# Rows by indirect DMA: a mixture of experts whose rows are fetched and summed in DRAM

## What is computed

```python
def swiglu(x, wg, wu, wd):
    return jnp.dot(jax.nn.silu(jnp.dot(x, wg)) * jnp.dot(x, wu), wd)

def moe_swiglu(x, router, wg, wu, wd):
    xf = x.reshape(-1, x.shape[-1])
    logits = jnp.dot(xf, router).astype(jnp.float32)
    top_v, top_i = lax.top_k(logits, TOP_K)
    probs = jax.nn.softmax(top_v, axis=-1)
    gate = jnp.sum(jax.nn.one_hot(top_i, N_EXPERTS) * probs[..., None], axis=1)
    y = jnp.zeros(xf.shape, jnp.float32)
    for e in range(N_EXPERTS):
        y = y + gate[:, e:e + 1] * swiglu(xf, wg[e], wu[e], wd[e])
    return y
```

## Time and profile before

| | |
|---|---|
| median of 3 runs | 1292.19 us (1291.65 to 1292.32) |
| the profiled execution | 1290.74 us, its span 1289.0 us |
| PE busy | 96% |
| DVE busy | 79% |
| ACT busy | 64% |
| DMA, mean | 258 GB/s |
| mean granted PE clock | 0.986 of full speed |

### The profile page before, as it was taken

One profiled execution on the slowest core, in us unless ns is written; L12 is line 12 of the kernel. 1 busy time (PEld: TensorE's weight loads), 2 busy tenths in 40 slices (PEclk: granted clock), 3 DMA queues, 4 the chain that ended last, 5 costly groups with the idle time before them and its releaser, 6 DMA issues.

```text
span 1289.0 us, 16501 instructions
## 1 busy us (share of the span) xinstructions
PE 1231.6 (96%) x6719; PEld 1066.7 (83%) x6719; DVE 1012.1 (79%) x977; ACT 818.6 (64%) x899; POOL 4.2 (0%) x20
## 2 busy tenths in 40 slices
PE   6999999999998899999999999999999999999993
PEld 4899999989998778878887887887887887887882
DVE  6687444457997678889889879879879979879875
ACT  3646563345776577767776776776776767767751
POOL 0000000000000000000000000000000000000000
PEclk8999999999999999999999999999999999999996
DMA  9145543434463169989998998998998998998931
GB/s 254 45 154 163 164 163 131 164 98 131 144 215 121 64 232 371 372 298 356 371 327 322 371 328 320 371 331 326 372 321 329 372 335 312 373 338 311 370 143 52
DMA packets 167645, 333.03 MB, mean 258 GB/s; under 512 B 6404, under 2 KB 58980, under 8 KB 167530
## 3 DMA queue, kind: packets, MB, share of 16 engines
q1 hardware_dynamic: 167363, 331.28, 72.9%
q10 hardware_dynamic: 199, 0.62, 0.2%
HBM read 330.44 MB, written 2.84 MB: 259 GB/s over the span
## 4 chain that ended last, share of the span: by engine, by line
PE 75%; DVE 20%; ACT 3%; issue 1%; DMA 0%; DVEq 0%; SPq 0%; ACTq 0%
PE bank L1145 29%; PE bank L1167 17%; PE bank L961 17%; DVE w_lo L1247 10%; PE bank L992 6%; DVE cacc L1430 2%; PE bank L1098 2%; ACT w_hi L569 1%; PE bank L1154 1%; PE bank L900 1%; DVE acc L1595 1%; DVE yy_lo L1665 1%; PE bank L946 1%; DVE sg L1327 1%; DMA xin<-in_x_prompt_dram 0%
## 5 line engine op out<-in xcount | busy, mean ns | idle before, releaser
L1247 DVE TENSOR_TENSOR w_lo<-raw,w_hi 128x2048 fp32r<-128x2048 f32 x309 | 703.7, 2289 | 145.6 <-ACT w_hi L569 145.4
L569 ACT CAST w_hi<-raw 128x2048 fp32r<-128x2048 f32 x309 | 590.1, 1918 | 251.7 <-PE bank L1145 93.7
L1145 PE MATMUL bank<-w_hi,xg_hi 128*128 128x512 f32 (+1 forms) x768 | 290.6, 378 | 1.1 <-DVE xg_lo L1602 1.1
L1145 PE MATMUL bank<-w_lo,xg_hi 128*128 128x512 f32 (+1 forms) x768 | 287.2, 374 | 0.0
L1145 PE MATMUL bank<-w_hi,xg_lo 128*128 128x512 f32 (+1 forms) x768 | 286.8, 373 | 0.0
L961 PE MATMUL bank<-x_hi,w_hi 128*128 128x304 f32 (+1 forms) x544 | 165.8, 305 | 6.9 <-DVE x_lo L1334 3.7
L1145 PEld LDWEIGHTS bank<-w_hi,xg_hi 128*128 128x128 f32 x768 | 144.7, 188 | 27.6 <-issue 1.3
L1145 PEld LDWEIGHTS bank<-w_hi,xg_lo 128*128 128x128 f32 x768 | 144.5, 188 | 26.7
L1145 PEld LDWEIGHTS bank<-w_lo,xg_hi 128*128 128x128 f32 x768 | 144.9, 189 | 25.2
L961 PE MATMUL bank<-x_hi,w_lo 128*128 128x304 f32 (+1 forms) x544 | 163.8, 301 | 0.0
L961 PE MATMUL bank<-x_lo,w_hi 128*128 128x304 f32 (+1 forms) x544 | 163.1, 300 | 0.0
(11 more groups left out here) (197 smaller groups left out, 1227.7 us busy)
## 6 DMA issues: line engine op xcount, KB each, us to landing
raw<-in_moe_w_gate_dram SPq DMA_DIRECT2D x88, 1024.0 KB, 5.4
raw<-in_moe_w_up_dram SPq DMA_DIRECT2D x88, 1024.0 KB, 5.4
raw<-in_moe_w_down_dram SPq DMA_DIRECT2D x88, 1024.0 KB, 5.3
raw<-in_conv_w_dram SPq DMA_DIRECT2D x12, 1024.0 KB, 5.5
raw<-in_ffn_w_gate_dram SPq DMA_DIRECT2D x11, 1024.0 KB, 5.3
raw<-in_ffn_w_up_dram SPq DMA_DIRECT2D x11, 1024.0 KB, 5.3
raw<-in_ffn_w_down_dram SPq DMA_DIRECT2D x11, 1024.0 KB, 4.9
poolw<-in_pool_w_dram SPq DMA_DIRECT2D x1, 1024.0 KB, 10.9
```

The lines of the kernel that those rows point to most:

```text
L569: act.copy(w_hi[t % HIGH][:], raw[raw_slot(t)][:]).then_inc(hi_ready, 1)
L1145: done = pe.matmul(bank[:, 0:w], x[:, f, :], m[:, c, :], start=(f == 0 and k == 0), stop=(f == KC - 1 and k == 2))
L1247: dve.tensor_tensor(w_lo[raw_slot(t)][:], raw[raw_slot(t)][:], w_hi[t % HIGH][:], ALU.subtract).then_inc(split_ready, 1)
```

## The change

- Rows are stored once, as `xn` in float32 (no hi and lo), to a DRAM tensor `rows_dram`, and `acc` (alpha times the rows) to `sums_dram`, which has 128 more rows for slots that no row fills. Both are stored by SP ahead of the load of expert tile 11.
- `sel` is made for all experts before the first one, in three parts. `find_rows` multiplies it with `gate`, whose columns are now a 1, the shares of the 8 experts and the row's number: each slot gets its row's number, its share, and whether it is filled. DVE turns these into `row_in` (row to fetch), `row_out` (row to add to) and `share`.
- For each expert, GpSimd fetches 128 rows by an indirect DMA into `xg_rows`. `gather_rows` and ACT's copies go; `gather_turn` waits for the DMA.
- `scatter`, `sel_t`, the splits of `yy` and the adds on DVE go. ACT writes `yy`, the result times `share`, and GpSimd adds it to the rows of `sums_dram` by an indirect DMA that accumulates. It is issued behind the fetch of the next expert but one, and each add waits for the one before. The last expert is left out.
- In the last expert, behind its last weight tile, SP loads `g_row`, `b_row` and the sums of the seven experts into `acc`; DVE and ACT norm all rows, at places in block 4, block 5 and behind, and SP stores all outputs. For the last expert's own slots GpSimd fetches the sums to `z_rows`; DVE adds `yy` times share, norms these 128 rows, and two indirect stores (one to each output, with a bound that drops the other's rows) write them over what SP stored.
- PE's last `down` finishes its first half (bank 6) six matmuls ahead of the second. ACT reads the flag before the first expert.

```diff
+            def store_rows():
+                for i in range(3):
+                    n = OUT_ROWS[i]
+                    sp.wait_ge(rows_copied, 2 * i + 2)
+                    sp.dma_start(rows_dram[P * i:P * i + n, :], xn[0:n, i, :]).then_inc(rows_stored, 16)
+                for i in range(3):
+                    n = OUT_ROWS[i]
+                    sp.wait_ge(acc_ready, 2 * i + 2)
+                    sp.dma_start(sums_dram[P * i:P * i + n, :], acc[0:n, i, :]).then_inc(sums_stored, 16)
+                sp.dma_start(sums_dram[NM:NM + P, :], acc[:, 0, :]).then_inc(sums_stored, 16)
...
+            def fetch(n, e):
+                pool.indirect_dma_start(xg_rows[:], None, rows_dram, rows(row_in[:, e:e + 1], 0)).then_inc(xg_landed, 16)
+
+            def add(n, e):
+                pool.wait_ge(yy_done, 2 * n + 2)
+                pool.indirect_dma_start(sums_dram, rows(row_out[:, e:e + 1], 0), yy[:], None,
+                                        compute_op=ALU.add).then_inc(added, 16)
+
+            pool.wait_ge(rows_stored, 48)
+            pool.wait_ge(in_ready, 1)
+            fetch(0, 0)
+            pool.wait_ge(in_ready, 3)
+            for e in range(1, E):
+                pool.wait_ge(gathered, 2 * e)
+                fetch(e, e)
+                if e == 2:
+                    pool.wait_ge(sums_stored, 64)
+                    pool.wait_ge(out_ready, 1)
+                elif e > 2:
+                    pool.wait_ge(added, 16 * (e - 2))
+                if e > 1:
+                    add(e - 2, e - 2)
+            pool.wait_ge(added, 16 * (E - 2))
+            add(E - 2, E - 2)
+            pool.wait_ge(added, 16 * (E - 1))
+            pool.wait_ge(rows_stored, 48)
+            pool.indirect_dma_start(z_rows[:], None, sums_dram, rows(row_out[:, E - 1:E], 0)).then_inc(z_landed, 16)
...
+            pool.wait_ge(y_stored, 48)
+            pool.wait_ge(rows_ready, 1)
+            pool.indirect_dma_start(y_prompt[0], rows(row_out[:, E - 1:E], 0), y_rows[:], None,
+                                    bounds_check=SEQ - 1, oob_is_err=False).then_inc(y_placed, 16)
+            pool.indirect_dma_start(y_sample.rearrange("b t d -> (b t) d"), rows(row_ys[:], 0), y_rows[:], None,
+                                    bounds_check=NS - 1, oob_is_err=False).then_inc(y_placed, 16)
...
+            def find_rows(r, k):
+
+                e0, e1, bank = FINDS[k]
+                pe.wait_ge(sel_ready, r * len(FINDS) + (k + 1))
+                for e in range(e0, e1):
+                    for i in range(3):
+                        n = OUT_ROWS[i]
+                        last = pe.matmul(ps[bank][:, GC * e:GC * (e + 1)], sel[0:n, e, i, :], gate[0:n, i, :],
+                                         start=(i == 0), stop=(i == 2))
+                last.then_inc(rows_found, 1)
...
                     rows_block(ps[2 + (j + 1) % 2], j, g + halves(j))
-                    if j == 1 and scatters:
-                        pe.wait_ge(summed, scattered + 4)
+                    if j == 1 and (not isinstance(n, int) or n > 0):
+                        pe.wait_ge(yy_done, n * 2)
                     if j:
-                        if j == NB - 1 and not last:
-                            gather_rows(n + 1)
                         down(j - 1, g + 2 * halves(j))
...
+                    if kept and j == NB - 1:
+                        for i in range(2):
+                            rows_center(0, i)
                     mult(j)
...
+                    if kept and j == NB - 2:
+                        dve.wait_ge(sums_loaded, 48)
+                        for i in range(3):
+                            rows_stats(0, i)
+                        dve.wait_ge(rows_landed, 32)
+                if kept:
+                    rows_center(0, 2)
+                    for i in range(2):
+                        rows_scale(0, i)
                 turn_low(NB - 1)
+                if kept:
+                    rows_scale(0, 2)
...
+            def last_rows():
+
+                dve.wait_ge(z_landed, 16)
+                for k in range(2):
+                    cols = slice(k * HALF, (k + 1) * HALF)
+                    if k == 0:
+                        dve.wait_ge(first_half, E)
+                    else:
+                        dve.wait_ge(tile_used, T_MOE + E * TE)
+                    dve.scalar_tensor_tensor(out=yy[:, cols], in0=ps[6 + k][:, :], scalar=share[:, E - 1:E],
+                                             in1=z_rows[:, cols], op0=ALU.mult, op1=ALU.add).then_inc(yy_done, 1)
...
```

More of the change, by code:

```diff
@@ L510, in _ @@
                     one_pass(r)
[L511 to L520, removed]
+                sp.wait_ge(added, 16 * 3 * E)
+                load_sums()
+                store_y(1)
+                sp.wait_ge(y_stored, 16 * 6)
             sp.wait_ge(u_stored, 16 * (1 + ST_))
-            sp.wait_ge(stored, 16 * (4 + 3))
+            sp.wait_ge(stored, 16 * 4)
+            sp.wait_ge(y_stored, 16 * 3)
+            sp.wait_ge(y_placed, 32)
         @block.gpsimd
@@ L554, in _ @@
+        N_CONSTS = 13
         @block.scalar
@@ L785, in one_expert @@
                 t0 = n * TE
+                kept = last and isinstance(r, int)
                 m0 = T_MOE + side * TE
@@ L857, in _ @@
                     one_pass(r)
[L859 to L862, removed]
+                all_rows_std(1)
         @block.tensor
@@ L1110, in gather_turn @@
                     last.then_inc(gathered, 1)
-            def scatter(y_count):
-                pe.wait_ge(yy_lo_done, y_count)
-                for k in range(6):
-                    i, half = k // 2, k % 2
-                    n = OUT_ROWS[i]
-                    for m, y in enumerate((yy_hi, yy_lo)):
-                        last = pe.matmul(ps[SCATTER_BANKS[k]][0:n, :], sel_t[:, P * i:P * i + n],
-                                         y[:, half * HALF:(half + 1) * HALF], start=(m == 0), stop=(m == 1))
-                    last.then_inc(spread, 1)
             def one_expert(r, first, side, last):
@@ L1577, in _ @@
             link(last)
+            for i in range(3):
+                last = dve.scalar_tensor_tensor(out=slot_of[:, i, 0:E], in0=ps[1][:, i * E:(i + 1) * E], scalar=1.0,
+                                                in1=taken[:, i, :], op0=ALU.add, op1=ALU.mult)
             for i in range(3):
@@ new lines, in _, with rows_stats, rows_center @@
+            output_rows(0)
+            def rows_stats(k, i):
+                n = OUT_ROWS[i]
+                for half in range(2):
+                    dve.bn_stats(stats[0:n, i, half, :],
+                                 acc[0:n, i, half * HALF:(half + 1) * HALF]).then_inc(fin_half, 1)
+                dve.wait_ge(fin_half, 6 * k + 2 * i + 2)
+                dve.bn_aggr(mv[0:n, i, :], stats[0:n, i, :, :].rearrange("p a b -> p (a b)")).then_inc(fin_stats, 1)
+            def rows_center(k, i):
+                n = OUT_ROWS[i]
+                dve.wait_ge(fin_stats, 3 * k + i + 1)
+                dve.scalar_tensor_tensor(out=acc[0:n, i, :], in0=acc[0:n, i, :], scalar=mv[0:n, i, 0:1],
+                                         in1=g_row[0:n, :], op0=ALU.subtract, op1=ALU.mult).then_inc(fin_g, 1)
@@ L1609, in one_expert @@
                 n = pair + side
-                e = first + side
-                scatters = not isinstance(n, int) or n > 0
                 m0 = T_MOE + side * TE
+                kept = last and isinstance(r, int)
                 def ahead(j):
```

367 lines of the change are left out of this document (208 added, 159 removed).

## The result

The changed kernel takes 1249.18 us (1248.36 to 1249.45) where the kernel before took 1291.92: a ratio of 0.9669, with a 95% interval of 0.9653 to 0.9686, or 42.7 us less. The forecast was 1234, the range 1226 to 1256. The profiled execution has 1249.45 us and a span of 1247.7.

A forecast was written before the change was run, and what follows sets the result against it. PE, busy 96% of the span, was taken as the bound. 1290.7 - 49.0 (loop) + 2.7 (start) + 2.0 (last expert) - 15.6 (tail) + 2 (DMA) = 1232.8, with the runs' median 1.45 higher: 1234 us, range 1226 to 1256.

The forecast's parts named there:

- rival 1: Expert loop: DMA becomes the bound at 371 GB/s, +16 to +24 us, about 1254; chance 0.11.
- Rival 3: Start and tail: GpSimd's indirect DMAs cost several us each to issue, three on the path at +7, 1255; chance 0.07.
- What leaves PE in the loop: Expert loop: scatter 29.3 us and gather 19.2 us leave PE, sum 49.0; an expert takes 94.5 us.
- DMA: Expert loop: 36.2 MB an expert needs 383 GB/s; +2 us taken, bounds 0 to +24.
- rival 2: Expert loop: DMA ceiling at 364 GB/s, 99.4 us an expert, +31 us, 1265; chance 0.04.
- The start: Ahead of the first expert matmul: DVE makes `row_in`, then the fetch lands; +2.7 us, bounds -0.1 to +4.8.
- 450.4 + 6.4 + 2.15 = 459.0: Start: `row_in` written at 450.4, fetch 6.4 us, transposes to first expert matmul 2.15 us, so that matmul at 459.0.
- The last expert: Last expert: DVE's norm work on all rows delays the last `ht_lo` from 1259.9 to 1261.8, +2.0 us in all.
- The tail: After the last `down` matmul: 4.4 us of DVE and 6.1 of indirect stores, 10.5 us instead of 26.05, -15.6.
- Rival 4: Expert transitions: the weight splits are late at each, 7 x 1.5 = +10 us, 1244; chance 0.05.
- Rival 5: Expert loop: the accumulating add holds the weight stream, 11 us over the cushion, 7 times, +77, 1311; chance 0.04.

The follow-up runs named there:

- e4_no_adds: Changed kernel with its seven indirect accumulating DMAs each replaced by a plain 1 KB DMA with the same waits: 1249.86 us, ratio 0.967.
- e3_after_no_busy: Changed kernel without the eight idle matmuls behind `find_rows`: 1248.66 us, ratio 0.966.
- e5_five_fetches: Changed kernel, large tensors at their old places, each fetch of experts 1 to 6 issued five times, four into unused space: 1247.77 us, ratio 0.9684.
- e1_before_moved32: Kernel before, with only its large working tensors moved by 32 bytes in each partition: 1298.73 us, ratio 1.0052.

## Why the prediction came out as it did

**The total: inside the range, by luck in part.** The forecast's own bounds ended at 1243; up to 1256 the range was widened for rivals 1 and 3, and neither came true. 1249.18 lies in the range because of costs that no term and no rival named.

**What leaves PE in the loop: right.** With the places held equal, an expert went from 101.4 to 94.48 us, and 4.18 + 2.74 us had been read off PE's timeline as what leaves.

**The size that was missed: the step of the matmuls that stay.** The sum took over 0.229 us a matmul for what the change does not touch. It did not follow that one tensor of two columns, put ahead of the large ones, moves every operand but the weight tiles by 32 bytes. That cost 11.7 us: the two loops, 768.6 us after and 756.9 at the old places, differ by 11.7, and so do the medians. Of the 2.05 us lost ahead of the experts it explains 0.9; the rest is within what that point does from one execution to the next: the traces with the same places and the same code up to there reach it at 447.98 (`e4_no_adds`) to 450.10 (`e3_after_no_busy`). The prediction named no such term, and none of its rivals has this cause; the slowdown that rival 1 would have given (+16 to +24) looks alike in the total but not in the trace.

**DMA: the right side, for a good reason.** +2 had been put in and nothing was lost. The ceiling of 371 of rival 1 and of 364 of rival 2 are both refuted by 388 GB/s in `e5_five_fetches`. The argument that the old rates were set by PE, and so floors, was the right one. The limit of about 358 GB/s of the Trainium skill's "DMA: Bandwidth & Descriptors", section Specifications, is not seen here either: this case's trace has 388 over 95 us on a single core. But the estimate of 383 GB/s needed was near (375 to 381 in the windows), and the margin proved small.

**The start: the wrong work was on the path.** The forecast followed DVE and the fetch. Both were nearly right: `row_in` was written at 452.14, or 450.1 by the old timeline, against 450.4, and the fetch took 5.3 us to land, against 6.4, though it was issued 0.9 us after `row_in` was done. But the forecast priced only DVE's part of making `row_in`, and nothing of PE's queue between the fetch's issue and the transposes: 42 more records of `find_rows` at 0.25 us, 10.4 us at the lower clock, and eight idle matmuls, 3.5 us. The transposes began at 466.03, 7.5 us after the fetch had landed. The step that failed is "450.4 + 6.4 + 2.15 = 459.0": by the old timeline it was 466.1, 7.1 later. The diff shows both in PE's program, ahead of `one_pass(0)`.

**The last expert: right in kind, half in size.** PE waited 1.06 us for the last `ht_lo`. But it had waited 0.92 us there before, and the forecast of 2.0 came on top of that (before, then after):

```profile
1259.92 0.50 PE L1167 MATMUL bank<-w_hi,ht_hi 128*128 128x512 f32 x1 [0.92 <-DVE ht_lo L1627]
```
```profile
1233.64 0.50 PE L1267 MATMUL bank<-w_hi,ht_hi 128*128 128x512 f32 x1 [1.06 <-DVE ht_lo L1739]
```

With an earlier wait of 0.3 us for `ht_lo` the waits grew by 0.45 us. By its length, at the old places, the last expert took 95.5 us, where 98.8 less the scatter's 4.2 gives 94.6: 0.9 us more, where 2.0 had been forecast.

**The tail: right.** 10.99 against 10.5 us: 4.5 for DVE (4.4), then 6.5 for the two indirect stores (6.1), of which 0.9 lies between DVE's end and the first issue. The first half's add did not run under PE's last matmuls as a whole, since the half itself was done only at 1235.4; it started there, at 1235.41.

**Rival 3 (GpSimd's issue)**: the eight fetches took 1.0 us each to issue, the first 1.84, an add 2.2; all but those of start and tail were hidden. **Rival 4 (late splits)**: no wait of PE for `w_lo` in the expert stage. **Rival 5 (the add holds the stream)**: an add lands in 9.9 us and takes none of PE's time, as `e4_no_adds` shows. What hides in the total is that three things made up for part of the misses: 1.9 us of clock in the first 72 matmuls (17.04 against 18.59 us in spite of the longer step), the 2 us set aside for DMA, and the 1 us of the last expert. The first is luck of the trace that the forecast started from, whose clock was low there; `e1_before_moved32` has 17.03 with the old code.

## What to carry over

When a change removes work from the engine that bounds, the subtraction from its timeline can be very good (94.45 against 94.48 us an expert here); what went wrong was what stays. Look in the diff for everything that shifts addresses, and compare the start-to-start step of an unchanged matmul before and after as the first reading. At a stage's start, write down the whole queue of the engine that must act when the awaited DMA lands: the DMA is the path only if that queue is empty by then. And look at the granted clock of the stretch that a forecast starts from: a low stretch may not be there in the next execution.

## What the runs showed of the hardware

- The step of a float32r matmul of 128 x 128 by 512 columns depends on the place of its stationary operand in the partition. At the three places tried it was 0.227 us (a multiple of 128 bytes), 0.229 (a multiple of 64 only) and 0.2333 (32 bytes off). With 304 columns and the moving operand 32 bytes off it went from 0.1391 to 0.1400.
- The granted clock fell while PE was busy without a gap: from full to a mean of 0.60 over 452 to 456 us, in the 48 records of `find_rows`, with 2 us of idle matmuls at full clock before them.
- Executions with the same code up to there differ in where the granted clock is low: the piece of 1056 dense matmuls took 149.63 us in one and 148.33 in another with the same places, with a clock of 0.67 and 1.00 over 48 to 52 us.
- Indirect DMAs of 128 rows of 4 KB: 0.95 to 1.0 us of GpSimd to issue a fetch (1.84 the first time), 4.1 to 6.3 us to land (kernel after), 5.3 for the first, which has no weight loads beside it; 2.2 us to issue an accumulating one and 9.9 us to land.
- One core, 1 MiB weight loads and such DMAs together: 388 GB/s was the most it kept up, in windows of 95 us with ACT waiting for loads.
